# Turning 32 rows of transition factors instead of 16 blocks of input matrix in a state-space preparation

## The chip, the cores and the metric

The kernel runs on one core of a Trainium2 chip. The metric is the device time of one execution in microseconds (us). TensorE is called PE here, VectorE DVE, ScalarE ACT, GpSimd POOL, SyncE SP; PEld is TensorE's weight load.

## The reference

Two layers (`l` = 0, 1) act on `x` [256 tokens, 1024]. Each layer is a SwiGLU feed-forward, a mixer and a second feed-forward, each added to the residual and normalised. The part around the change is the state-space branch of the mixer, cut here to what matters:

```python
def ssm_branch(u, lam_re, lam_im, log_dt, b_re, b_im, c_re, c_im, d_skip, w_glu):
    ...
    dt = jnp.exp(log_dt.astype(f32))[:, None]
    a_bar = jnp.exp(lam * dt)
    b_bar = ((a_bar - 1.0) / lam)[:, :, None] * lax.complex(b_re.astype(f32), b_im.astype(f32))
    c_mat = lax.complex(c_re.astype(f32), c_im.astype(f32))
    bu = jnp.einsum('blgh,gph->blgp', u32.astype(jnp.complex64), b_bar)
    ...
    _, states = lax.associative_scan(combine, (a_seq, bu), axis=1)
    y = jnp.einsum('blgp,ghp->blgh', states, c_mat).real \
        + d_skip.astype(f32).reshape(N_GROUPS, SSM_GROUP) * u32
```

There are 32 groups of 16 channels with 64 complex states each. A complex number takes two planes (`v` = 0 real, 1 imaginary). `a` is `a_bar` and `g` is the step factor `(a_bar - 1) / lam`, one of each per state.

## The kernel before, in words

All weights stream from HBM in tiles of 128x1024 f32. SP loads them into four `raw` slots; ACT makes the high part `whi` (L450) and DVE the remainder `wlo` (L1289), in rings of eight tiles. PE multiplies high by high, high by low and low by high (L777 to L779 and L835, L839). A slot of the ring comes free when PE has used the tile (`pe_used`).

A feed-forward has 11 up chunks (`feature_chunk`, four tiles each) and then a down stage of 22 tiles. When PE has done a chunk, ACT and DVE sum, gate and split it. Their order is written out by hand and has four splits of later weight tiles in it: DVE L1289 twice (the pair), L1327, L1330, L1289, L1335, L1289, L1340; the last one increments `h_split`. The chunks use two sets of PSUM banks, and the last chunk (number 10) lies in banks 0, 1, 6 and 7. The down stage sums in banks 2 to 5; its step `k` is 12 matmuls of 128x512, for both halves of the tokens, and begins while ACT and DVE still work on chunk 10. It is followed by `late_pass`, the normalisation and the transposition of `x` for the next stage.

The constants of the state-space branch are made during the feed-forward ahead of the mixer that uses them: during the first feed-forward of layer 0 for layer 0, and during the second feed-forward of layer 0 for layer 1 (`prepare(l)` on POOL). POOL computes `a` and `g` in [128 states, 16] form, then for four quarters `q` the input matrix `b_bar = g*b` and the product `a*b_bar`, then `a*c`, each by `cmul` (six operations of 128x128). Then it doubles the tables `tab_c` and `tab_s` of cosines and sines seven times; the last two stages work on 128x512 elements at a time, into the scratch tile `h`. `op` (L1709) issues a POOL operation and lets POOL wait for it. After `prepare`, the same queue computes `rstd` (L1733), which the normalisation waits for.

The state input product `ssm_in` needs these matrices with the channels on the partitions. So in the down stage, after step `k` = 5 (`TURN_B_AT`), PE turns 16 blocks of 128x128 (`turn_b`, L965) into banks 0, 1, 6, 7, after a wait for `h_split` of chunk 10; ACT copies them to `b_t` in four pieces (L502). After step 9 (`DIRECT_AT`), PE makes the term `c*b_bar` of even steps in 32 small products (`direct_terms`, L976), which DVE copies to `k0_t` (L1428).

Of the kernel before, what the change touches and what calls it, by code (L numbers as in the profile page):

```python
# [13 lines left out]
P = 128  # L14
# [89 lines left out]
def build(nc, A, out):  # L104
# [65 lines left out]
    b_bar = place("b_bar", [P, NQ, 2, P])  # L170
# [40 lines left out]
    bias_rows = nc.dram_tensor("bias_rows", (N_HEADS, 512), F32, kind="Internal").ap()  # L211

# [6 lines left out]
    for name in ("first_landed first_hi first_lo hi_done split_done pe_used rest_done ident_landed const_landed affine_landed const_ready tok_ready "  # L219
                 "xt_done xh_done x_ready up_done silu_done h_ready ht_done hh_done h_split acc_done "  # L220
                 "var_ready rstd_ready dve_chain pool_chain out_done bias_built bias_stored "
                 "tab_ready gate_low up_low gate_sum gate_silu up_sum up_h par_landed b_landed c_landed d_landed lam_ready "
                 "angle_ready sincos_ready bbar_ready bt_done bt_ready ct_ready k0_done k0_ready ca_ready "
                 "proj_done proj_read pt_done pt_read bu_done bu_read decay_ready scan_done states_ready y_used "
                 "idx_done relu_done weighted idx_added mask_ready mask_set s_done neg_max_ready exp_done prt_done prt_read "
                 "pv_done inv_ready prob_ready yah_done ya_split bra_read y_sum gelu_done yh_done y_split gm_done "
                 "tanh_done glu_ready ysh_done ys_split brs_done bra_done merged_ready mt_done mh_done m_split").split():
        S[name] = sem(name)
# [101 lines left out]

    def bar(q, v):

        return b_bar[:, q, v, :] if v < 2 else b_raw[:, v - 2, 4 * q:4 * q + 4, :].rearrange("p j n -> p (j n)")
# [6 lines left out]
    with block:  # L340
# [102 lines left out]
        def _(act):  # L443
# [70 lines left out]
            def ffn(f, s0, prep):  # L514
                for c in range(OLD_C):
                    token_chunk(f, s0 + 4 * c, c)
                    if c == 1 and prep is not None:
                        prepare_angles(prep)
                h_hi(f, OLD_C - 1)
                for c in range(OLD_C, PEEL):  # L520
                    feature_chunk(0, f, s0 + 4 * c, c, c % 2)
                with act.Fori(0, LOOP_I) as i:
                    for e in range(2):
                        feature_chunk(i, f, s0 + 4 * (PEEL + e), 2 * i + PEEL + e, (PEEL + e) % 2)
                for k in range(HK - RING):
                    splits(s0 + UP_Q + RING + k, 1)
                    if prep is not None and TURN_B_AT <= k < TURN_B_AT + NQ:
                        prepare_b(prep, k - TURN_B_AT)
# [245 lines left out]
        def _(pe):  # L774
# [146 lines left out]
            def late_pass(f, s, k0, n, ah, al, stage, prep):  # L921
# [37 lines left out]
            def turn_b(l, f):  # L959

                pe.wait_ge(S["bbar_ready"], NQ * (l + 1))
                pe.wait_ge(S["h_split"], steps(f, NC_UP - 1) + 1)
                for q in range(NQ):
                    for v in range(4):
                        ins = nc.tensor.transpose(ps[:, TURNED_B[q], v * P:v * P + P], bar(q, v), ident[:, :])  # L965
                    ins.then_inc(S["bt_done"], 1)

            def direct_terms(l):

                pe.wait_ge(S["bt_ready"], NQ * (l + 1))  # L970
                pe.wait_ge(S["ct_ready"], l + 1)
                for q in range(NQ):
                    for v in range(2):
                        for r in range(4):
                            rows = slice(32 * r, 32 * r + 32)
                            ins = nc.tensor.matmul(ps[rows, 0, 32 * q:32 * q + 32], b_bar[:, q, v, rows],  # L976
# [3 lines left out]
            def ffn(f, stage, s0, following, prep):  # L980
# [11 lines left out]
                for k in range(HK - RING):  # L992
# [21 lines left out]
            def ssm_in(l, half):  # L1014

                if half == 0:
                    pe.wait_ge(S["pt_read"], 4 * l + 2)
                    pe.wait_ge(S["bt_ready"], NQ * (l + 1))
# [253 lines left out]
        def _(dve):  # L1272
# [145 lines left out]
            def negate_c(l):  # L1418

                dve.wait_ge(S["c_landed"], 16 * (l + 1))  # L1420
                nc.vector.tensor_scalar(c_t[:, 1, :, :], c_t[:, 1, :, :], -1.0, None, ALU.mult
# [10 lines left out]
            def ffn(f, s0, prep):  # L1432
# [12 lines left out]
                for k in range(HK - RING):  # L1445
                    splits(s0 + UP_Q + RING + k, 1)
                    if prep is not None and k == DIRECT_AT:
                        prepare_k0(prep)
# [251 lines left out]
        def _(pool):  # L1700
# [48 lines left out]
            def prepare(l):  # L1749
# [28 lines left out]
                pool.dma_start(c_t[:, 0:2, :, :], A["ssm_c_rows"][l]).then_inc(S["c_landed"], 16)  # L1778
# [7 lines left out]
                def cmul(dr, di, ar_, ai_, br, bi, sign=1, done=None):  # L1786

                    nc.gpsimd.tensor_tensor(dr, ar_, br, ALU.mult)
                    op(product, ai_, bi, ALU.mult)
                    op(dr, dr, product, ALU.subtract if sign == 1 else ALU.add)  # L1790
                    nc.gpsimd.tensor_tensor(di, ar_, bi, ALU.mult)
                    op(product, ai_, br, ALU.mult)
                    op(di, di, product, ALU.add if sign == 1 else ALU.subtract, done)
# [3 lines left out]

                def prepare_b(q):

                    js = slice(4 * q, 4 * q + 4)  # L1800

                    def bb(v):
                        return bar(q, v).rearrange("p (j n) -> p j n", j=4)

                    cmul(bb(0), bb(1), col(16, js), col(17, js), b_raw[:, 0, js, :], b_raw[:, 1, js, :])
                    cmul(bb(2), bb(3), col(11, js), col(12, js), bb(0), bb(1), 1, S["bbar_ready"])
                    pool.wait_ge(S["bbar_ready"], NQ * l + q + 1)
# [47 lines left out]
                while n < HALF:  # L1855
# [71 lines left out]
TURN_B_AT, DIRECT_AT = 5, 9  # L1927
TURNED_B = [0, 1, 6, 7]
# [5 lines left out]
def ssm_layout(inputs):  # L1934
# [15 lines left out]

    log_dt = np.broadcast_to(np.asarray(inputs["ssm_log_dt"]).reshape(DEPTH, NJ, 2).transpose(0, 2, 1)[:, :, None, :],
# [3 lines left out]
    return {"ssm_params": params, "ssm_d_cols": d_cols, "ssm_b_rows": blocks("ssm_b_re", "ssm_b_im"),  # L1955
# [46 lines left out]
```

## Time and profile before

| what | value |
|---|---|
| time, median of 3 runs | 1106.94 us (1106.74 to 1107.53) |
| the profiled execution's own time | 1107.71 us |
| its span | 1105.9 us |
| granted TensorE clock | 0.998 |
| PE, DVE, ACT, POOL busy | 99%, 71%, 53%, 35% of the span |
| PE in the chain that ended last | 91% of the span |
| HBM read | 207.02 MB, 188 GB/s over the span |

Matmuls overlap in the pipeline, so a row of PE has a duration of 0.39 us while the next one starts 0.23 us later. Costs on PE are read from the differences of start times. "Busy" of DVE and POOL holds the time in which an operation stands still in the engine.

### The profile page before, as it was taken

To read this page: it belongs to the slowest core of one execution; us is meant where nothing else is said; L and a number is where in the kernel's file an instruction comes from. 1 tells how busy PE (TensorE), PEld (TensorE's weight loads), DVE (VectorE), ACT (ScalarE), POOL (GpSimd) and SP (SyncE) were. 2 spreads that over 40 slices of the span, in tenths; PEclk is the share of its full clock that TensorE was granted. 3 is DMA by queue.
4 is the path that set the end of the run, shared out by engine and by line. 5 is a ranking of instruction groups with operands and counts; after the bars stand their busy time and mean duration, and the time that the engine had idled before them with its cause. 6 is when DMAs were issued, how large, how long until landed. Compare 5 with 4: busy or idle time off the path is not lost.

```text
span 1105.9 us, 18440 instructions
## 1 busy us (share of the span) xinstructions
PE 1095.6 (99%) x6411; PEld 929.5 (84%) x6411; DVE 780.6 (71%) x1085; ACT 586.6 (53%) x841; POOL 384.2 (35%) x536
## 2 busy tenths in 40 slices
PE   9999999999999999999999999999999999999997
PEld 7888888997788888888888888889877888888886
DVE  6766676789978866777576667477897787566744
ACT  6555543574873555555345555336748645555540
POOL 3989893107600289989000000011274000000001
PEclk9999999999999999999999999999999999999999
DMA  9866763744575576666466666636545666657651
GB/s 291 269 186 203 253 209 113 229 121 130 158 229 190 173 252 194 190 219 216 124 204 198 183 209 210 224 92 211 168 123 153 209 199 211 192 182 214 204 183 38
DMA packets 158655, 208.96 MB, mean 189 GB/s; under 512 B 12760, under 2 KB 107128, under 8 KB 158592
## 3 DMA queue, kind: packets, MB, share of 16 engines
q1 hardware_dynamic: 155232, 202.29, 57.8%
q10 hardware_dynamic: 2592, 3.67, 1.3%
q0 software_dynamic: 768, 2.17, 0.5%
q8 instruction: 38, 0.62, 0.2%
q14 instruction: 25, 0.20, 0.1%
HBM read 207.02 MB, written 1.06 MB: 188 GB/s over the span
## 4 chain that ended last, share of the span: by engine, by line
PE 91%; DVE 4%; issue 2%; ACT 2%; DMA 1%; POOLq 0%; POOL 0%; DVEq 0%; SPq 0%; ACTq 0%
PE ps L835 24%; PE ps L777 15%; PE ps L779 15%; PE ps L778 15%; PE ps L839 12%; DVE wlo L1289 2%; PE ps L849 1%; PE ps L1166 1%; DMA raw<-in_w_in 1%; PE ps L1168 1%; PE ps L1169 1%; PE ps L791 1%; PE ps L1029 1%; DVE score L1503 1%; PE ps L1081 1%
## 5 line engine op out<-in xcount | busy, mean ns | idle before, releaser
L1289 DVE TENSOR_TENSOR wlo<-raw,whi 128x1024 fp32r<-128x1024 f32 (+1 forms) x371 | 470.0, 1287 | 199.0 <-ACT whi L450 196.1
L450 ACT CAST whi<-raw 128x1024 fp32r<-128x1024 f32 (+1 forms) x371 | 377.4, 1043 | 226.1 <-PE ps L779 134.3
L835 PE MATMUL ps<-x_hl,whi 128*128 128x512 f32 x1152 | 362.5, 396 | 0.0
L839 PEld LDWEIGHTS ps<-x_hl,wlo 128*128 128x128 f32 x1152 | 216.4, 188 | 51.1
L839 PE MATMUL ps<-x_hl,wlo 128*128 128x256 f32 x1152 | 226.5, 278 | 0.0
L1733 POOL TENSOR_TENSOR rstd<-var_eps,cst 128x1 f32<-128x1 f32 x12 | 18.3, 1527 | 542.3 <-DVE var_eps L1355 533.2
L835 PEld LDWEIGHTS ps<-x_hl,whi 128*128 128x128 f32 x1152 | 175.7, 189 | 0.3
L777 PE MATMUL ps<-whi,x_hl 128*128 128x512 f32 (+1 forms) x400 | 156.6, 392 | 0.0
L778 PE MATMUL ps<-wlo,x_hl 128*128 128x512 f32 (+1 forms) x400 | 153.1, 383 | 0.0
L779 PE MATMUL ps<-whi,x_hl 128*128 128x512 f32 (+1 forms) x400 | 153.1, 383 | 0.0
L777 PE MATMUL ps<-whi,hh 128*128 128x512 f32 (+1 forms) x355 | 138.2, 389 | 0.0
L779 PE MATMUL ps<-whi,hl 128*128 128x512 f32 (+1 forms) x355 | 137.5, 387 | 0.0
L778 PE MATMUL ps<-wlo,hh 128*128 128x512 f32 (+1 forms) x355 | 137.5, 387 | 0.0
L777 PEld LDWEIGHTS ps<-whi,x_hl 128*128 128x128 f32 x400 | 75.1, 188 | 17.1 <-issue 3.6
L779 PEld LDWEIGHTS ps<-whi,x_hl 128*128 128x128 f32 x400 | 75.1, 188 | 14.7
L778 PEld LDWEIGHTS ps<-wlo,x_hl 128*128 128x128 f32 x400 | 75.2, 188 | 13.4
L779 PEld LDWEIGHTS ps<-whi,hl 128*128 128x128 f32 x355 | 66.7, 188 | 13.6
L777 PEld LDWEIGHTS ps<-whi,hh 128*128 128x128 f32 x355 | 66.7, 188 | 13.4
L778 PEld LDWEIGHTS ps<-wlo,hh 128*128 128x128 f32 x355 | 66.7, 188 | 13.2
L486 ACT COPY silu<-ps 128x512 f32<-128x512 f32 x36 | 21.1, 587 | 79.1 <-PE ps L839 79.1
L492 ACT CAST hh<-ps 128x512 f32 (+1 forms) x36 | 21.1, 588 | 73.3 <-DVE ps L1335 73.3
L1709 POOL TENSOR_TENSOR small<-small 128x16 f32<-128x16 f32 x102 | 48.2, 472 | 7.9
(206 smaller groups left out, 1370.8 us busy)
## 6 DMA issues: line engine op xcount, KB each, us to landing
raw<-in_ffn_w_up SPq DMA_DIRECT2D x351, 256.0 KB, 3.6
raw<-in_ffn_w_down SPq DMA_DIRECT2D x176, 256.0 KB, 3.3
raw<-in_w_in SPq DMA_DIRECT2D x128, 256.0 KB, 3.4
raw<-in_w_branch SPq DMA_DIRECT2D x32, 256.0 KB, 3.2
raw<-in_w_out SPq DMA_DIRECT2D x32, 256.0 KB, 3.9
bias_g<-bias_rows ACTq DMA_DIRECT2D x16, 192.0 KB, 3.9
raw<-in_w_in SPq DMA_DIRECT2D x16, 148.0 KB, 2.2
affine<-in_ln_g SPq DMA_DIRECT2D x4, 512.0 KB, 5.9
```

What stands on the lines that cost most here:

```text
L450: nc.scalar.copy(whi[:, s % RING, 0:w], raw[:, s % RAW, 0:w]).then_inc(S["hi_done"], 1)
L486: nc.scalar.copy(silu[:, :, :], halves(b, 0)[1]).then_inc(S["gate_low"], 1)
L492: nc.scalar.copy(hh[:, bass.ds(2 * c, 2), :], halves(b, 1)[0]).then_inc(S["hh_done"], 1)
L777: nc.tensor.matmul(o, ah, bh, start=start, stop=False)
L778: nc.tensor.matmul(o, ah, bl, start=False, stop=False)
L779: return nc.tensor.matmul(o, al, bh, start=False, stop=stop)
L791: ins = nc.tensor.transpose(ps[:, XT[i] + half, (k % 4) * P:(k % 4 + 1) * P], x[:, i, k * P:(k + 1) * P], ident[:, :])
L835: nc.tensor.matmul(ps[:, bank, :], w(whi, s + q, at, at + P), x_hl[:, k, :, :], start=k == 0, stop=False)
L839: ins = nc.tensor.matmul(ps[:, bank, 0:SEQ], w(wlo, s + q, at, at + P), xh[:, k, :], start=False, stop=k == KT - 1)
L1289: nc.vector.tensor_tensor(wlo[:, s % RING, 0:w], raw[:, s % RAW, 0:w], f32(whi[:, s % RING, 0:w]), ALU.subtract).then_inc(S["split_done"], 1)
L1709: ins = nc.gpsimd.tensor_tensor(o, a, b, f)
L1733: nc.gpsimd.tensor_tensor(rstd[:, i, :], var_eps[:, i, :], cst[:, 0:1], ALU.pow).then_inc(S["rstd_ready"], 1)
```

## The change: what it does

The step factor `g` goes to the output matrix: `g*c` takes the place of `c`, and the raw `b` that of `b_bar`. So the direct terms need no input matrix made by POOL. `b` is passed a second time by the host, already turned (`ssm_b_cols`, 512 KB a layer), and loaded straight into `b_t`. Of the products, `a*b` is still needed in turned form: POOL writes `a` (16 columns real, 16 imaginary) into `tmp`, PE turns that once, ACT copies the 32 rows and stores them in HBM (`a_rows`, 16 KB), and four DMAs from POOL's queue read them back, each to 32 partitions. POOL then multiplies in six operations of 128x512. The turn comes after step 2 of the down stage (`TURN_A_AT`), with the direct terms right behind it; DVE reads these after its split of step 3.

```diff
-                for q in range(NQ):
-                    for v in range(4):
-                        ins = nc.tensor.transpose(ps[:, TURNED_B[q], v * P:v * P + P], bar(q, v), ident[:, :])
-                    ins.then_inc(S["bt_done"], 1)
+                pe.wait_ge(S["a_ready"], l + 1)
+                pe.wait_ge(S["h_split"], steps(f, NC_UP - 1) + 1)
+                nc.tensor.transpose(ps[:, 1, 0:P], tmp[:, :], ident[:, :]).then_inc(S["at_done"], 1)
...
-                    if prep is not None and k == TURN_B_AT:
-                        turn_b(prep, f)
-                    if prep is not None and k == DIRECT_AT:
+                    if prep is not None and k == TURN_A_AT:
+                        turn_a(prep, f)
                         direct_terms(prep)
...
-                pe.wait_ge(S["bt_ready"], NQ * (l + 1))
-                pe.wait_ge(S["ct_ready"], l + 1)
+                pe.wait_ge(S["b_landed"], 16 * (l + 1))
+                pe.wait_ge(S["cg_ready"], NQ * (l + 1))
...
-                        pe.wait_ge(S["bt_ready"], NQ * (prep + 1))
+                        pe.wait_ge(S["at_read"], prep + 1)
...
-            def prepare_b(l, q):
-                act.wait_ge(S["bt_done"], NQ * l + q + 1)
-                nc.scalar.copy(b_t[:, q, :, :], ps[:, TURNED_B[q], :].rearrange("p (v n) -> p v n", v=4)
-                               ).then_inc(S["bt_ready"], 1)
+            def store_a(l):
+                act.wait_ge(S["at_done"], l + 1)
+                nc.scalar.copy(tmp[0:2 * NJ, :], ps[0:2 * NJ, 1, 0:P]).then_inc(S["at_read"], 1)
+                act.wait_ge(S["at_read"], l + 1)
+                act.dma_start(a_rows, tmp[0:2 * NJ, :]).then_inc(S["a_stored"], 16)
...
+                pool.dma_start(b_t[:, :, 0:2, :], A["ssm_b_cols"][l]).then_inc(S["bc_landed"], 16)
...
-                pool.wait_ge(S["b_landed"], 16 * (l + 1))
                 pool.wait_ge(S["ct_ready"], l + 1)
                 for q in range(NQ):
-                    prepare_b(q)
-                for q in range(NQ):
                     js = slice(4 * q, 4 * q + 4)
-                    cmul(c_t[:, 2, js, :], c_t[:, 3, js, :], col(11, js), col(12, js), c_t[:, 0, js, :],
-                         c_t[:, 1, js, :], -1, S["ca_ready"])
-                    pool.wait_ge(S["ca_ready"], NQ * l + q + 1)
+                    cmul(c_t[:, 0, js, :], c_t[:, 1, js, :], col(16, js), col(17, js), c_t[:, 2, js, :],
+                         c_t[:, 3, js, :], product, -1, S["cg_ready"])
+                    pool.wait_ge(S["cg_ready"], NQ * l + q + 1)
+                op(tmp[:, 0:NJ], ar, k(14), ALU.mult)
+                op(tmp[:, NJ:2 * NJ], ai, k(14), ALU.mult, S["a_ready"])
...
+                pool.wait_ge(S["tab_ready"], l + 1)
+                pool.wait_ge(S["a_stored"], 16 * (l + 1))
+                for r in range(4):
+                    src = bass.AP(a_rows.tensor, r * P, [[0, 32], [NJ * P, 2], [4 * P, NQ], [1, P]])
+                    pool.dma_start(at_t[32 * r:32 * r + 32, :, :, :], src).then_inc(S["a_landed"], 16)
+                for q in range(NQ):
+                    js = slice(4 * q, 4 * q + 4)
+                    cmul(c_t[:, 2, js, :], c_t[:, 3, js, :], col(11, js), col(12, js), c_t[:, 0, js, :],
+                         c_t[:, 1, js, :], product, -1, S["ca_ready"])
+                    pool.wait_ge(S["ca_ready"], NQ * l + q + 1)
+                pool.wait_ge(S["a_landed"], 64 * (l + 1))
+                pool.wait_ge(S["bc_landed"], 16 * (l + 1))
+                t = h[:, 1, :, :].rearrange("p t n -> p (t n)").rearrange("p (q n) -> p q n", q=NQ)
+                cmul(b_t[:, :, 2, :], b_t[:, :, 3, :], at_t[:, 0, :, :], at_t[:, 1, :, :], b_t[:, :, 0, :],
+                     b_t[:, :, 1, :], t, 1, S["bt_ready"])
...
-TURN_B_AT, DIRECT_AT = 5, 9
-TURNED_B = [0, 1, 6, 7]
+TURN_A_AT, READ_K0_AT = 2, 3
```

How instructions move, first on PE, in the down stage of the feed-forward that holds the preparation. Before, step 5 is followed by:

```order
L779 MATMUL ps<-whi,hl 128x512
L965 MATMUL ps<-ident,b_bar 128x128 [waits h_split,bbar_ready]
L965 MATMUL ps<-ident,b_bar 128x128
L965 MATMUL ps<-ident,b_raw 128x128 x2
...
L777 MATMUL ps<-whi,hh 128x512 [waits split_done]
...
L976 MATMUL ps<-c_t,b_bar 32x32 [waits ct_ready,bt_ready]
L976 MATMUL ps<-c_t,b_bar 32x32 x31
```

where the last two rows follow step 9. With the change, step 2 is followed by:

```order
L777 MATMUL ps<-whi,hl 128x512
L961 MATMUL ps<-ident,tmp 128x128 [waits h_split,a_ready]
L971 MATMUL ps<-c_t,b_raw 32x32 [waits cg_ready,b_landed]
L971 MATMUL ps<-c_t,b_raw 32x32 x31
L775 MATMUL ps<-whi,hh 128x512 [waits split_done]
```

The wait for `h_split` has moved ahead by three steps, the small products by seven. On POOL, in `prepare`, the last table operation was followed at once by `rstd`:

```order
L1868 TENSOR_TENSOR tab_s<-tab_c,small 128x8x64 [waits pool_chain]
L1709 TENSOR_TENSOR h<-tab_s,small 128x512
L1709 TENSOR_TENSOR tab_s<-tab_s,h 128x8x64 [waits pool_chain]
L1733 TENSOR_TENSOR rstd<-var_eps,cst 128x1 [waits var_ready] x2
L1709 TENSOR_TENSOR h_st<-spare 128x16 [waits tok_ready]
```

and now stand between them (the 24 operations of `a*c` shortened to their first two):

```order
L1703 TENSOR_TENSOR tab_s<-tab_s,h 128x8x64 [waits pool_chain]
L1863 DMA at_t<-a_rows 32x8x128 [waits a_stored,tab_ready]
L1863 DMA at_t<-a_rows 32x8x128 x3
L1783 TENSOR_TENSOR c_t<-small,c_t 128x128
L1703 TENSOR_TENSOR tmp<-small,c_t 128x128
...
L1783 TENSOR_TENSOR b_t<-at_t,b_t 128x4x128 [waits bc_landed,a_landed,ca_ready]
L1703 TENSOR_TENSOR h<-at_t,b_t 128x512
L1703 TENSOR_TENSOR b_t<-b_t,h 128x4x128 [waits pool_chain]
L1786 TENSOR_TENSOR b_t<-at_t,b_t 128x4x128 [waits pool_chain]
L1703 TENSOR_TENSOR h<-at_t,b_t 128x512
L1703 TENSOR_TENSOR b_t<-b_t,h 128x4x128 [waits pool_chain]
L1727 TENSOR_TENSOR rstd<-var_eps,cst 128x1 [waits var_ready] x2
```

Ahead of the tables, POOL's 72 operations of 128x128 have become 24, so that the tables start earlier, and work that was ahead of them now lies behind.

## Rows read from the trace of the kernel before

**Rows 1.** The page's busy time, share of the span and instructions of each engine.
```profile
PE 1095.6 (99%) x6411; PEld 929.5 (84%) x6411; DVE 780.6 (71%) x1085; ACT 586.6 (53%) x841; POOL 384.2 (35%) x536
```
**Rows 2.** The longest wait of PE: line, releaser: us in total, times, longest.
```profile
PE ps L1259 <- DVE k_t L1662: 1.3, 1, 1.3
```
**Rows 3.** Timeline of PE, layer 0, around the 16 transpositions: start us, duration us.
```profile
146.16 0.38 PE L965 MATMUL ps<-ident,b_bar 128*128 128x128 f32 x2
...
147.83 0.47 PE L777 MATMUL ps<-whi,hh 128*128 128x512 f32 x1
```
**Rows 4.** Timeline of PE, layer 0, around the direct terms.
```profile
158.92 0.76 PE L976 MATMUL ps<-c_t,b_bar 128*32 128x32 f32 x64
159.62 0.51 PE L777 MATMUL ps<-whi,hh 128*128 128x512 f32 x1
```
**Rows 5.** Timeline of PE, the end of step 2: layer 0, then layer 1's preparation.
```profile
137.99 0.39 PE L777 MATMUL ps<-whi,hh 128*128 128x512 f32 x1
...
499.68 0.39 PE L777 MATMUL ps<-whi,hh 128*128 128x512 f32 x1
```
**Rows 6.** Timeline of DVE on chunk 10, layer 0; in brackets the idle time before.
```profile
128.93 2.62 DVE L1289 TENSOR_TENSOR wlo<-raw,whi 128x1024 fp32r<-128x1024 f32 x2
131.47 0.69 DVE L1327 TENSOR_TENSOR ps<-ps,silu 128x512 f32<-128x512 f32 x1
...
137.48 1.49 DVE L1289 TENSOR_TENSOR wlo<-raw,whi 128x1024 fp32r<-128x1024 f32 x1 [1.71 <-ACT whi L450]
138.89 0.68 DVE L1340 TENSOR_TENSOR hl<-ps,hh 128x512 f32 x1
```
**Rows 7.** The same of layer 1's preparation.
```profile
489.25 2.90 DVE L1289 TENSOR_TENSOR wlo<-raw,whi 128x1024 fp32r<-128x1024 f32 x2
...
494.63 2.02 DVE L1289 TENSOR_TENSOR wlo<-raw,whi 128x1024 fp32r<-128x1024 f32 x1 [1.00 <-ACT whi L450]
...
498.96 2.06 DVE L1289 TENSOR_TENSOR wlo<-raw,whi 128x1024 fp32r<-128x1024 f32 x1 [1.71 <-ACT whi L450]
500.95 0.68 DVE L1340 TENSOR_TENSOR hl<-ps,hh 128x512 f32 x1
```
**Rows 8.** DVE L1289, ns min/median/max, in 60:142, 142:175 and 494:528 us.
```profile
L1289 DVE TENSOR_TENSOR wlo<-raw,whi x31: 1207/1297/1485, 60.3 to 141.8; 128x1024 fp32r<-128x1024 f32 x31
L1289 DVE TENSOR_TENSOR wlo<-raw,whi x12: 1225/1516/2266, 141.8 to 172.0; 128x1024 fp32r<-128x1024 f32 x12
L1289 DVE TENSOR_TENSOR wlo<-raw,whi x13: 1228/1750/2311, 494.6 to 525.5; 128x1024 fp32r<-128x1024 f32 x13
```
**Rows 9.** Timeline of POOL, layer 0: products, tables, `rstd`.
```profile
63.73 0.40 POOL L1788 TENSOR_TENSOR b_bar<-small,b_raw 128x128 f32<-128x128 f32 x1
...
96.82 0.40 POOL L1788 TENSOR_TENSOR c_t<-small,c_t 128x128 f32<-128x128 f32 x1
...
112.34 0.24 POOL L1865 TENSOR_TENSOR tab_c<-tab_c,small 128x16 f32<-128x16 f32 x1
...
156.11 1.05 POOL L1865 TENSOR_TENSOR tab_c<-tab_c,small 128x512 f32<-128x512 f32 x1
...
174.16 1.29 POOL L1709 TENSOR_TENSOR tab_s<-tab_s,h 128x512 f32<-128x512 f32 x1
183.70 1.54 POOL L1733 TENSOR_TENSOR rstd<-var_eps,cst 128x1 f32<-128x1 f32 x1 [8.24 <-DVE var_eps L1355]
```
**Rows 10.** The same of layer 1's preparation: first and last table operation.
```profile
463.65 0.23 POOL L1865 TENSOR_TENSOR tab_c<-tab_c,small 128x16 f32<-128x16 f32 x1
...
525.11 1.30 POOL L1709 TENSOR_TENSOR tab_s<-tab_s,h 128x512 f32<-128x512 f32 x1
```
**Rows 11.** POOL's issue of one DMA: count | us in all, mean ns | idle before.
```profile
L1778 POOL DMA_DIRECT2D c_t<-in_ssm_c_rows x2 | 1.1, 538 | 0.0
```
**Rows 12.** DMA issues of POOL: KB each, median us to landing.
```profile
c_t<-in_ssm_c_rows POOLq DMA_DIRECT2D x2, 512.0 KB, 7.4
bias_rows<-bias_sb POOLq DMA_DIRECT2D x1, 16.0 KB, 4.7
```

More of the change, by code:

```diff
@@ L169, in build @@
     b_raw = place("b_raw", [P, 2, NJ, 32])
-    b_bar = place("b_bar", [P, NQ, 2, P])
+    at_t = place("at_t", [P, 2, NQ, P])
     tmp = place("tmp", [P, P])
@@ L211, in build @@
     bias_rows = nc.dram_tensor("bias_rows", (N_HEADS, 512), F32, kind="Internal").ap()
+    a_rows = nc.dram_tensor("a_rows", (2 * NJ, P), F32, kind="Internal").ap()
     raw_landed = [sem(f"raw_landed{i}") for i in range(RAW)]
@@ L526, in ffn @@
                     splits(s0 + UP_Q + RING + k, 1)
-                    if prep is not None and TURN_B_AT <= k < TURN_B_AT + NQ:
-                        prepare_b(prep, k - TURN_B_AT)
+                    if prep is not None and k == TURN_A_AT:
+                        store_a(prep)
             def proj_read(l, c, t):
@@ L975, in direct_terms @@
                             rows = slice(32 * r, 32 * r + 32)
-                            ins = nc.tensor.matmul(ps[rows, 0, 32 * q:32 * q + 32], b_bar[:, q, v, rows],
+                            ins = nc.tensor.matmul(ps[rows, 0, 32 * q:32 * q + 32], b_raw[:, v, 4 * q + r, :],
                                                    c_t[:, v, 4 * q + r, :], start=v == 0, stop=v == 1)
@@ L996, in ffn @@
                     ins.then_inc(S["pe_used"], 1)
-                    if prep is not None and k == TURN_B_AT:
-                        turn_b(prep, f)
-                    if prep is not None and k == DIRECT_AT:
+                    if prep is not None and k == TURN_A_AT:
+                        turn_a(prep, f)
                         direct_terms(prep)
@@ L1017, in ssm_in @@
                     pe.wait_ge(S["pt_read"], 4 * l + 2)
-                    pe.wait_ge(S["bt_ready"], NQ * (l + 1))
+                    pe.wait_ge(S["bt_ready"], l + 1)
                     pe.wait_ge(S["proj_read"], 2 * NPROJ * l + 4)
@@ L1420, in negate_c @@
                 dve.wait_ge(S["c_landed"], 16 * (l + 1))
-                nc.vector.tensor_scalar(c_t[:, 1, :, :], c_t[:, 1, :, :], -1.0, None, ALU.mult
+                nc.vector.tensor_scalar(c_t[:, 3, :, :], c_t[:, 3, :, :], -1.0, None, ALU.mult
                                         ).then_inc(S["ct_ready"], 1)
@@ L1446, in ffn @@
                     splits(s0 + UP_Q + RING + k, 1)
-                    if prep is not None and k == DIRECT_AT:
+                    if prep is not None and k == READ_K0_AT:
                         prepare_k0(prep)
@@ L1784, in prepare, with cmul @@
                 product = tmp[:, :].rearrange("p (j n) -> p j n", j=4)
-                def cmul(dr, di, ar_, ai_, br, bi, sign=1, done=None):
+                def cmul(dr, di, ar_, ai_, br, bi, t, sign=1, done=None):
                     nc.gpsimd.tensor_tensor(dr, ar_, br, ALU.mult)
-                    op(product, ai_, bi, ALU.mult)
-                    op(dr, dr, product, ALU.subtract if sign == 1 else ALU.add)
+                    op(t, ai_, bi, ALU.mult)
+                    op(dr, dr, t, ALU.subtract if sign == 1 else ALU.add)
                     nc.gpsimd.tensor_tensor(di, ar_, bi, ALU.mult)
-                    op(product, ai_, br, ALU.mult)
-                    op(di, di, product, ALU.add if sign == 1 else ALU.subtract, done)
+                    op(t, ai_, br, ALU.mult)
+                    op(di, di, t, ALU.add if sign == 1 else ALU.subtract, done)
                 def col(n, js):
                     return m(n)[:, js].unsqueeze(2).to_broadcast([P, 4, 32])
[L1798 to L1807, printed above, removed]
                 def square(dr, di, sr, si_):
@@ L1949, in blocks, with turned @@
         return rows.reshape(DEPTH, P, 2, NJ, 2 * SSM_GROUP)
+    def turned(rows):
+        return rows.reshape(DEPTH, P, 2, NQ, 4, 32).transpose(0, 4, 5, 3, 2, 1).reshape(DEPTH, P, NQ, 2, P)
+    b_rows = blocks("ssm_b_re", "ssm_b_im")
     log_dt = np.broadcast_to(np.asarray(inputs["ssm_log_dt"]).reshape(DEPTH, NJ, 2).transpose(0, 2, 1)[:, :, None, :],
```

11 lines of the change are left out of this document (4 added, 7 removed).

## The prediction

> **What bounds the kernel now.** I read the page's busy shares first: PE is busy for 99% of the span [rows 1]. Then the list of waits: the longest wait of PE in the whole execution is 1.3 us, and that is at the start [rows 2]. So PE sets the end in every stage, whatever ACT, DVE and POOL do beside it. An edit is worth what it takes from PE's own queue, less each moment in which it makes PE wait where it did not wait before. The next views are therefore timelines: PE's at the place of the edit, then those of the engines that release the wait which has moved there, and last POOL's, whose work is moved about.
>
> **What PE saves.** The first transposition starts at 146.16 us and the next weight product at 147.83 [rows 3]. That is 1.67 us, and the product behind them takes 0.47 us where the others take 0.39 or 0.40, 0.08 more. So 16 transpositions cost 1.75 us, 0.11 us each, and one is left: 1.64 us less for each layer, 3.3 us for both. The direct terms (0.70 us from their start to that of the next product, [rows 4]) keep their number and shapes and only move; I cost that at nothing. Their inputs are there: `g*c` is done by about 80 us (below) and needed at 138.
>
> **What the moved wait costs.** Both the old and the new turn wait for `h_split` of chunk 10, because they write to a bank that chunk 10 fills. DVE's last operation on that chunk starts at 138.89 us and takes 0.68, so the chunk is split at 139.57 [rows 6]. The old turn at 146.16 found it long done. The new one stands behind step 2, which is issued in full when step 3 starts in the old trace, at 137.99 us [rows 5]. As it is, PE would stand for 139.57 - 137.99 = 1.6 us. In layer 1's preparation the chunk is split at 500.95 + 0.68 = 501.63 [rows 7] and step 2 ends at 499.68 [rows 5]: 1.95 us. Queued behind that wait on PE are the direct terms and all weight products; nothing can go past it. I add 0.2 us each time for the restart, since the transposition's weight load can't be hidden under a running product; no row shows this, the spacing of transpositions (0.11 us) is a bound from below and a product of 0.39 one from above.
>
> **How POOL changes these two waits.** In front of the tables, POOL has 48 operations fewer: the block of `b` products ran from 63.73 to 96.82 us, 33.1 us, and is gone; the block of `c` products (96.82 to 112.34, 15.5 us) is replaced by one of `g*c` of the same shapes [rows 9]. New are two operations of 128x16 and one DMA issue of 0.54 us [rows 11], about 1.1 us together. So all tables come 32 us earlier. Their last stage, on tiles of 128x512, ran from 156.11 to 175.45 and will run from about 124 to 143.5, right over the chain of chunk 10. In layer 1's preparation the tables ended at 525.11 + 1.30 = 526.4 [rows 10] and will end at 494.4, near the middle of that chain.
>
> This matters because DVE's splits are slower beside such POOL operations: the median of L1289 is 1.30 us before 142 us, and 1.52 and 1.75 us in the two stretches with large table operations, up to 2.27 and 2.31 [rows 8]. In layer 0 five splits lie on the path to `h_split` from 126 us on: one of chunk 9, the pair ahead of L1327 (2.62 us together, and L1327 starts when DVE is free of it), and two inside the chain, 1.49 us for the last of them [rows 6]. They take about 1.4 us each now. At 1.65, between the two medians, they take 0.26 more each, 1.3 in all: the wait is 1.6 + 1.3 = **2.9 us**. The bounds are 1.6 (no split is slower) and 1.6 + 5 x 0.65 = 4.8 (each takes 2.02 to 2.06, as the two of rows 7 do).
>
> In layer 1's preparation it is the other way round for two of them: the two splits inside the chain took 2.02 and 2.06 us beside large POOL operations [rows 7] which will be over. At 1.30 they give back 1.5 us, while the pair ahead (2.90 us) and the one before it take some 0.5 more. That is 1.95 + 0.5 - 1.5 = 0.95. POOL's end (494.4) is close to the first of the two (494.63), so part of its share may stay; I take **1.2 us**, with bounds of 0.5 and 2.3 (the pair at 2.0 each, +1.1, and only the second split freed, -0.75).
>
> **What lies beside.** POOL must not be late for `rstd`. After the tables it waits for the store of `a`: turn at about 141, copy, a store that by the one small store in the trace lands 4.7 us after issue [rows 12], so 147. Four issues at 0.54 [rows 11] are 2.2, `a*c` is 15.5 again, and six operations of 128x512 are half of the last table stage (19.3 us for twelve), 9.7. End: 174.4 us, where the tables ended at 175.45 and POOL then sat idle for 8.24 us until 183.70 [rows 9]. The read-back has the 15.5 us of `a*c` to land, against 7.4 us for 512 KB [rows 12]. So the DMA detour costs nothing, as long as this gap of 9 us holds. ACT loses four copies and gets a small one and an issue; PE waits for it nowhere. DVE's read of the direct terms stands behind its split of step 3's ring slot, which comes after the terms are done. The added load of 512 KB a layer competes with weight tiles for some 2 us; splits run eight tiles ahead of PE, so I cost it at nothing, with 0.5 us as its upper end.
>
> **The sum.** -3.3 + 2.9 + 1.2 + 2 x 0.2 = **+1.2 us**, on the profiled execution's own 1107.7 us: 1108.9. The median of the three runs is 0.8 below that execution, so as a median it is 1106.94 + 1.2, some 1108.2 us. A measurement of this kernel can tell about 0.2% (2.2 us) from no change, so this counts as no change.
>
> The Trainium skill (SBUF — State Buffer, Who interferes with whom) says that a DVE instruction with two SBUF inputs contends with a POOL instruction that reads SBUF, through one shared read interface that is held as a lock. L1289 has two such inputs, and rows 8 agree in kind: it stretches to 2.3 us, and not only slightly. Taken as a lock on each of the five splits, the rule would make the time that of rival 2.
>
> **The rivals.**
> 1. *The wait is short* (18%). The splits keep their durations, since POOL and DVE happen to alternate: waits of 1.6 and 0.5 us, restart 0.3. Sum -3.3 + 2.4 = -0.9: 1106.0 us. For it: the minimum beside large operations is 1.23 us in both stretches [rows 8]. Against: the medians.
> 2. *Every split stands behind a POOL operation* (16%). Waits of 4.8 and 2.3, restart 0.4. Sum +4.2: 1111.1 us, slower. The place is chunk 10 in layer 0, and it decides from about 3.9 us there on, when the sum passes 2.2. For it: rows 7, where two of two splits took 2 us. Against: a median of 1.52 in the stretch that is moved here.
> 3. *The wait isn't one* (6%). `h_split` comes before step 2 is through, in both layers. Sum -3.3: 1103.7 us, faster. Against it stand both timelines, in which DVE is 1.6 and 1.95 us too late; it needs the change to speed up DVE ahead of both places, and it puts large POOL operations there in layer 0.
> 4. *POOL is late for `rstd`* (5%). If the four broadcast reads cost POOL 5 us each in place of 0.54, or land after 26 us in place of 7.4, the gap of 9 us is used up, and each further us is lost twice, once a layer. At 5 us over it is 10 us: about 1118 us. Nothing like this stands in the rows.
>
> The change could also fail to do what it says: POOL's total work hardly falls (72 small operations become 48, plus six large ones). But that isn't on PE's path, so it decides nothing.
>
> **How the numbers follow.** The forecast has 55%, with 1106.5 to 1110.5 as its own range; 8 of these 55 lie over +2.2 us. Slower by over 0.2%: 16 + 5 + 8 and a rounding = 30%. Faster by over 0.2%: rival 3 and 2% for a short wait that is shorter still: 8%. Within 0.2%: 62%. The range from 1106.0 to 1111.5 takes in the forecast and the greater part of rivals 1 and 2 and leaves out 3 and 4, nearly 2 in 10.
>
> **What would show it.** PE's timeline after step 2 must show a gap ahead of the transposition, released by DVE's split of chunk 10, near 3 us in layer 0 and 1 us in the next; the waits of PE must have a new group of about 4 us. The 16 rows of L965 must have become one of 0.1 us. L1289 must be slower between 126 and 139 us than before, and the large table operations must lie there. POOL must be idle before `rstd` as before. If the gap in layer 0 is 1.6 us or less, the step on DVE's splits is wrong; if PE waits at the transposition of `x`, rival 4 holds; if PE's gap is right and the time is not, the price of the transpositions is wrong.

## The result and the profile after

| | before | changed |
|---|---|---|
| time, median (lowest to highest) | 1106.94 us (1106.55 to 1107.53) | 1111.53 us (1110.11 to 1113.05) |
| profiled execution's own time, span | 1107.71, 1105.9 us | 1112.81, 1111.0 us |

The ratio of the times is 1.0041 [1.0032, 1.0050]: the changed kernel is slower by 4.6 us, which is more than the 0.2% that a measurement tells from no change. It lies at the upper edge of the forecast range (1111.5), 3.4 us above the forecast of +1.2, and in the case to which the prediction gave 30%. As a number it is nearest to rival 2 (1111.1 us), though that rival's waits were not met, as the rows below show. All seven executions are slower than every one before, and they spread over 2.9 us where those of before spread over 1.0.

The page's busy line and PE's longest waits, which answer to [rows 1] and [rows 2]:

```profile
PE 1095.7 (99%) x6381; PEld 928.8 (84%) x6381; DVE 786.6 (71%) x1085; ACT 583.3 (53%) x835; POOL 384.7 (35%) x514
```
```profile
PE ps L961 <- DVE hl L1334: 5.5, 2, 3.6
PE ps L1253 <- DVE k_t L1656: 1.3, 1, 1.3
```

30 of PE's instructions are gone, and yet its busy time is the same to 0.1 us. The new wait is the forecast one (`turn_a`, released by DVE's split of chunk 10), with 5.5 us where 4.1 was forecast. Something else must have made PE's instructions longer. The timeline of PE in layer 0 shows what; it answers to [rows 3] and [rows 5]:

```profile
138.00 0.39 PE L777 MATMUL ps<-whi,hl 128*128 128x512 f32 x1
141.95 0.30 PE L961 MATMUL ps<-ident,tmp 128*128 128x128 f32 x1 [3.57 <-DVE hl L1334]
142.18 1.06 PE L971 MATMUL ps<-c_t,b_raw 128*32 128x32 f32 x64
143.17 0.80 PE L775 MATMUL ps<-whi,hh 128*128 128x512 f32 x1
...
144.62 0.63 PE L775 MATMUL ps<-whi,hh 128*128 128x512 f32 x1
145.05 0.63 PE L776 MATMUL ps<-wlo,hh 128*128 128x512 f32 x1
...
146.02 0.39 PE L776 MATMUL ps<-wlo,hh 128*128 128x512 f32 x1
```

The next product was due at 138.23, so the gap is 3.72 us. Behind it the 32 small products take 0.99 us to the next start, where they took 0.70 [rows 4], and the weight products start 0.43 us apart instead of 0.23 until 145.5. The granted clock, in stretches of 4 us with PE's busy time, says why:

```profile
138.00:142.00 4.00, 0.43 (x3) 1.00 0.39 131
142.00:146.00 4.00, 4.00 (x72) 0.57 0.72 241
146.00:150.00 4.00, 4.00 (x19) 1.00 0.78 228
503.00:507.00 4.00, 2.03 (x71) 1.00 0.47 150
507.00:511.00 4.00, 4.00 (x11) 0.57 0.81 282
511.00:515.00 4.00, 4.00 (x19) 1.00 0.76 240
```

The columns are the stretch, PE's busy time with its instructions, the granted clock, the DMA share and GB/s. Behind each gap the clock is at its lower level (1.2 GHz in place of 2.4) for most of a stretch: 0.57 in the mean. In layer 0 it is low as soon as PE works again. In the other place the small products and the first weight products still run at full speed, and the slow ones begin 1.6 us after PE has started again. In the trace of before it is 1.00 in all six. In layer 1's preparation:

```profile
503.53 0.39 PE L777 MATMUL ps<-whi,hl 128*128 128x512 f32 x1
505.88 0.30 PE L961 MATMUL ps<-ident,tmp 128*128 128x128 f32 x1 [1.97 <-DVE hl L1334]
...
507.69 0.63 PE L775 MATMUL ps<-whi,hh 128*128 128x512 f32 x1
508.12 0.63 PE L776 MATMUL ps<-wlo,hh 128*128 128x512 f32 x1
```

Here the gap is 505.88 - 503.76 = 2.1 us. The lower clock costs 1.4 us in layer 0: 0.3 in the small products, and 1.1 in the weight products until they start 0.23 us apart again. Here it costs 1.6 us: eleven products take 4.20 us from 506.81 to 511.01, and eleven at full clock 2.6. When each instruction of PE is compared with the same one in the trace of before, PE falls back by 3.54 us at the first turn and 2.08 at the second. In both that is gap, plus slow stretch, less transpositions: 3.7 + 1.4 - 1.65 and 2.1 + 1.6 - 1.65, within 0.1. Some 0.5 us came before and between. 1.2 us is given back in layer 1's attention, where the profiled execution of before had a wait of 1.2 us that this one lacks. The sum is +5.0, and the profiled executions differ by 5.1.

Why the first gap is so long stands in DVE's timeline on chunk 10, which answers to [rows 6]:

```profile
127.07 1.23 DVE L1283 TENSOR_TENSOR wlo<-raw,whi 128x1024 fp32r<-128x1024 f32 x1 [1.71 <-ACT whi L447]
...
128.82 3.70 DVE L1283 TENSOR_TENSOR wlo<-raw,whi 128x1024 fp32r<-128x1024 f32 x2
...
134.72 2.14 DVE L1283 TENSOR_TENSOR wlo<-raw,whi 128x1024 fp32r<-128x1024 f32 x1 [1.00 <-ACT whi L447]
...
139.18 2.02 DVE L1283 TENSOR_TENSOR wlo<-raw,whi 128x1024 fp32r<-128x1024 f32 x1 [1.71 <-ACT whi L447]
141.12 0.68 DVE L1334 TENSOR_TENSOR hl<-ps,hh 128x512 f32 x1
```

Chunk 10 is split at 141.80, where it was split at 139.57: 2.2 us later. Read one by one, the five splits take 1.23 us (chunk 9), 1.47 and 2.31 (the pair, merged above into 3.70), 2.14 and 2.02. So three of the five take over 2 us. POOL's timeline beside them, which answers to [rows 9]:

```profile
135.86 1.91 POOL L1848 TENSOR_TENSOR tab_c<-tab_c,small 128x512 f32<-128x512 f32 x1
137.74 1.04 POOL L1703 TENSOR_TENSOR h<-tab_s,small 128x512 f32<-128x512 f32 x1
138.85 1.27 POOL L1703 TENSOR_TENSOR tab_c<-tab_c,h 128x512 f32<-128x512 f32 x1
140.20 1.90 POOL L1851 TENSOR_TENSOR tab_s<-tab_c,small 128x512 f32<-128x512 f32 x1
```

The large table operations lie over the chain as forecast, and they stretch in turn. Those that take 1.04 to 1.3 us where no split is beside them often take 1.9 to 2.3 where one is. The Trainium skill (SBUF — State Buffer, Who interferes with whom) describes such a lock between a two-input DVE instruction and POOL. The trace agrees in kind. Of the 44 splits of this execution that lie for most of their time beside POOL operations of 128x512, 8 take 1.2 to 1.3 us, 15 take 1.35 to 1.75 and 21 take 1.9 to 2.35. The 222 with no POOL operation beside them take 1.2.

### The profile page after: what moved, and what is told of

Read it like the earlier page. It is cut to its first block, busy times and chain, and to the rows that moved or that the text cites. A ratio compares the mean times of both kernels' runs of the same rounds, so it can differ in the third digit from the quotient of the medians.

```text
span 1111.0 us, 18356 instructions
## 1 busy us (share of the span) xinstructions
PE 1095.7 (99%) x6381; PEld 928.8 (84%) x6381; DVE 786.6 (71%) x1085; ACT 583.3 (53%) x835; POOL 384.7 (35%) x514
## 4 chain that ended last, share of the span: by engine, by line
PE 80%; DVE 7%; issue 5%; ACT 4%; DMA 3%; SPq 1%; DVEq 0%; POOLq 0%; POOL 0%; ACTq 0%
PE ps L833 20%; PE ps L775 14%; PE ps L777 14%; PE ps L776 14%; PE ps L837 10%; DVE wlo L1283 3%; ACT whi L447 2%; DMA raw<-in_ffn_w_down 2%; PE ps L1160 1%; DMA raw<-in_ffn_w_up 1%; PE ps L1162 1%; PE ps L1163 1%; PE ps L789 1%; PE ps L1023 1%; DVE score L1497 1%
## 5 line engine op out<-in xcount | busy, mean ns | idle before, releaser
L1283 DVE TENSOR_TENSOR wlo<-raw,whi 128x1024 fp32r<-128x1024 f32 (+1 forms) x371 | 476.2, 1304 | 207.1 <-ACT whi L447 204.5
L1896 POOL TENSOR_TENSOR h_st<-tab_c,gates 128x512 f32<-128x512 f32 x8 | 10.4, 1296 | 114.1 <-DVE wlo L1283 87.4
```

The lines of the kernel that those rows point to most:

```text
L1283: nc.vector.tensor_tensor(wlo[:, s % RING, 0:w], raw[:, s % RAW, 0:w], f32(whi[:, s % RING, 0:w]), ALU.subtract).then_inc(S["split_done"], 1)
```

## Experiments

All these kernels compute what the changed one does, or the one before. "PE gains" or "loses" is said of PE's instructions compared one by one with the same ones in the trace of before. The kernel before was run beside each: 1106.90 us (33 executions) for the first four, 1106.75 (29) for the others.

### The turn three steps later

```diff
-TURN_A_AT, READ_K0_AT = 2, 3
+TURN_A_AT, READ_K0_AT = 5, 6
```

> The changed kernel with the turn and the direct terms after step 5 of the down stage in place of step 2, nothing else. Theory A (the time was lost at the moved wait: a gap on PE, and behind it products at the lower of TensorE's two clocks): step 5 is issued at about 146.2 us, chunk 10 is split at 141.8, so there is no gap and no slow stretch; the time is that of before less 3.3 us, 1103.7 us, and the granted clock is 1.00 in every stretch of the down stage. Theory B (the added DMA load, the store and read-back, or POOL's new order cost PE something elsewhere): the time stays above 1105 us, and PE's waits or products show another place. The rival on POOL being late for rstd: POOL's chain starts some 4 us later than with step 2 and still ends about 3 us before rstd is wanted, so nothing is lost by either theory.

1104.94 us (1103.69 to 1106.46), ratio 0.9980 [0.9971, 0.9989]. Nothing waits at the turn, and the clock stays up. PE's timeline:

```profile
146.70 0.40 PE L777 MATMUL ps<-whi,hl 128*128 128x512 f32 x1
146.94 0.27 PE L961 MATMUL ps<-ident,tmp 128*128 128x128 f32 x1
147.14 0.76 PE L971 MATMUL ps<-c_t,b_raw 128*32 128x32 f32 x64
147.83 0.50 PE L775 MATMUL ps<-whi,hh 128*128 128x512 f32 x1
```

Turn and small products take 0.89 us together. PE gains 1.67 us at each of the two turns, 1.64 forecast. So the transpositions' price is right, and all that made the changed kernel slower than before hangs on the turn's place. The median falls by 1.96 us only, which misses the 1103.7 us expected by 1.2; the transpositions alone give 3.3. Of the rest the trace shows 0.8 us by which PE comes late to the first turn, 0.2 of it from a wait for chunk 9's split. That leaves about the 2.4 us by which the two profiled executions differ; why the medians lie 0.5 us closer stays open. The added DMA load and POOL's new order are in this kernel too, and it is faster than before: neither is what made the changed one slower by itself.

The same kernel was run again with the later ones, to compare within one chip:

> The turn after step 5 once more, to stand beside the kernel with the moved block of a*c on the same chip: 1104.9 us again, within 0.5 us.

1104.27 us (1103.34 to 1107.99), ratio 0.9981 [0.9973, 0.9990]: the same.

### The turn one step later

```diff
-TURN_A_AT, READ_K0_AT = 2, 3
+TURN_A_AT, READ_K0_AT = 3, 4
```

> The changed kernel with the turn after step 3. Step 3 is issued at 141.0 us in layer 0 and 506.5 in the other, chunk 10 is split at 141.8 and 505.7. Theory A: a gap of about 1 us in layer 0 and none in layer 1's preparation; time 1103.7 + 1 = 1104.7 us if so short a gap leaves the clock up, about 1106.2 if the clock falls behind it as it did behind 3.6 and 2.0 us. Theory B: no difference to the changed kernel beyond the gap, 1108 us or more.

1105.01 us (1103.85 to 1105.94), ratio 0.9980 [0.9970, 0.9989]. One step of twelve products, 2.7 us, is enough: no wait for chunk 10 is left, where one of about 1 us was expected in layer 0, and PE gains 1.64 and 1.67 us at the turns. DVE's timeline in layer 0 adds something to the reading above:

```profile
129.70 3.45 DVE L1283 TENSOR_TENSOR wlo<-raw,whi 128x1024 fp32r<-128x1024 f32 x2
135.35 1.22 DVE L1283 TENSOR_TENSOR wlo<-raw,whi 128x1024 fp32r<-128x1024 f32 x1 [1.00 <-ACT whi L447]
138.90 1.23 DVE L1283 TENSOR_TENSOR wlo<-raw,whi 128x1024 fp32r<-128x1024 f32 x1 [1.71 <-ACT whi L447]
```

The same two splits, in the same order of work on POOL, took 2.14 and 2.02 us in the profiled execution of the changed kernel and 1.2 here. Here the chunk is split at 140.72, 0.4 us before PE comes to the turn. A turn after step 2 would have stood 2.3 us. So the length of the gap in the changed kernel can be expected to differ from one execution to the next.

How long a turn after step 2 stands, or would stand, can be read in every trace, those of the later experiments too: it is the time from the end of step 2 to the split of chunk 10. The durations are those of single splits, the pair's two added.

| trace | layer 0: wait | pair, two splits inside the chain | layer 1's preparation: wait |
|---|---|---|---|
| before | 1.57 | 2.70, 1.42, 1.49 | 1.95 |
| wait alone | 1.35 | 2.69, 1.42, 1.47 | 1.15 |
| `a*c` ahead | 2.10 | 2.78, 1.41, 1.30 | 2.29 |
| both edits | 1.47 | 2.79, 1.41, 1.30 | 1.75 |
| changed | 3.57 | 3.78, 2.14, 2.02 | 1.97 |
| turn after step 5 | 2.56 | 3.52, 1.23, 1.23 | 1.99 |
| the same again | 3.64 | 3.77, 1.23, 2.05 | 1.67 |
| turn after step 3 | 2.32 | 3.52, 1.22, 1.23 | 1.98 |
| turn after step 8 | 3.68 | 3.76, 1.23, 2.05 | 1.67 |
| gap filled | 2.54 | 3.52, 1.23, 1.22 | 2.50 |

In the last six, with large table operations over the chain of layer 0, the wait is 2.3 to 3.7 us, 3.05 in the mean. The pair is slower in all six; the two splits inside the chain are slower in some only.

### The wait alone, in the kernel before

```diff
                     ins.then_inc(S["pe_used"], 1)
+                    if prep is not None and k == 2:
+                        pe.wait_ge(S["h_split"], steps(f, NC_UP - 1) + 1)
                     if prep is not None and k == TURN_B_AT:
```

> The kernel before with one wait added on PE: h_split of chunk 10 after step 2 of the down stage; transpositions and direct terms stay where they are. Theory A: gaps of 1.6 us in layer 0 and 2.0 us in layer 1's preparation plus restart, some 0.3 each, and if the clock falls behind such gaps another 1.5 us each: 1106.9 + 4.2 = 1111.1 us with the fall, 1111.1 - 3 = 1108 us without it. Theory B, by which the wait isn't what costs: within 0.1% of before, 1107 to 1108 us.

1109.95 us (1108.76 to 1112.95), ratio 1.0027 [1.0018, 1.0036]. The gaps are those of the old order of POOL:

```profile
138.59 0.39 PE L779 MATMUL ps<-whi,hl 128*128 128x512 f32 x1
140.22 0.50 PE L777 MATMUL ps<-whi,hh 128*128 128x512 f32 x1 [1.24 <-DVE hl L1342]
...
501.57 0.39 PE L779 MATMUL ps<-whi,hl 128*128 128x512 f32 x1
503.00 0.50 PE L777 MATMUL ps<-whi,hh 128*128 128x512 f32 x1 [1.04 <-DVE hl L1342]
```

The first product starts 1.40 and 1.20 us later than it was due, and it takes 0.11 us more until its successor starts. That makes 1.51 and 1.31, together 2.8 of the 3.05 us that the median shows. So the wait costs about 3 us without any change on POOL and with the transpositions as they were. The expected gaps were 1.6 and 2.0 us. In this execution the clock stays at 1.00 behind both. Two of the eleven executions lie 2 and 3 us above the median (1111.86 and 1112.95); the mean clock of the second is 0.997, of all others 0.998 or 0.999.

### `a*c` ahead of the last table stage

```diff
                 while n < HALF:
+                    if 2 * n == HALF:
...
+                        for q in range(NQ):
...
                     step = min(NJ, 4 * P // n)
...
-                for q in range(NQ):
...
                 pool.wait_ge(S["a_landed"], 64 * (l + 1))
```

> The changed kernel with POOL's block of a*c moved ahead of the last table stage (its scratch goes to h). Theory A with the contention of POOL and DVE: the large table operations start at 126 + 16 = 142 us in layer 0, behind the chain of chunk 10, so the splits there take 1.3 to 1.5 us as before the change and the gap shrinks from 3.7 to about 2 us; in layer 1's preparation they start at 494 us, over the chain, and the gap grows from 2.1 to about 3.3 us. The time hardly moves, 1110 to 1112 us; the two gaps are the test. If the contention is not the cause of the longer chain, both gaps stay as they are.

In the diff, `...` stands for the 24 operations of `a*c` and their scratch tile. 1108.08 us (1106.81 to 1110.79), ratio 1.0011 [1.0001, 1.0020]: 3.4 us less than the changed kernel, where hardly any difference (1110 to 1112 us) was expected. In layer 0 small POOL operations lie beside chunk 10. The pair takes 2.78 us, against 3.5 to 3.8 in the table above, and the splits inside the chain 1.41 and 1.30 (DVE's timeline):

```profile
135.35 1.41 DVE L1283 TENSOR_TENSOR wlo<-raw,whi 128x1024 fp32r<-128x1024 f32 x1 [1.00 <-ACT whi L447]
...
139.08 1.30 DVE L1283 TENSOR_TENSOR wlo<-raw,whi 128x1024 fp32r<-128x1024 f32 x1 [1.72 <-ACT whi L447]
```

The gaps are 141.12 - 138.88 = 2.24 us (3.72 in the changed kernel) and 504.98 - 502.54 = 2.44 (2.1). The second was expected to grow to 3.3. There the pair takes 3.98 us beside the large operations, but the two splits inside the chain are at 1.23. That these are short proves little by itself, since they are so beside large operations too in three rows of the table; the pair and the medians carry the reading. The two gaps also show that the clock doesn't follow from the length alone (PE, stretches of 4 us, columns as above):

```profile
138.00:142.00 4.00, 1.91 (x70) 1.00 0.43 150
142.00:146.00 4.00, 4.00 (x23) 0.59 0.81 275
502.00:506.00 4.00, 1.72 (x70) 1.00 0.49 154
506.00:510.00 4.00, 4.00 (x18) 1.00 0.80 251
```

The shorter gap is followed by the lower clock, the longer one isn't. The profiled execution is the slowest of the ten, 2.7 us above their median. Of the others three have a mean clock of 0.997 or less, and six 0.998 or more.

### Both edits

> The turn after step 5, and POOL's block of a*c ahead of the last table stage. Theory A with contention: with the turn at step 5 the trace lost 0.5 us before the down stage of layer 0, where PE waited for the split of chunk 9, which large POOL operations had made late; here these lie at 144 us and later, so that wait is gone and the time is 0.5 us under the kernel with the turn at step 5 alone, 1103.5 to 1104.5 us. If the 0.5 us was chance, both kernels take the same. POOL ends at about 181 us, still ahead of rstd's point of need (184 us); should it be late, PE waits at the transposition of x and the time is above that of the turn at step 5 alone.

The turn after step 5 and `a*c` ahead of the last stage: 1103.91 us (1103.16 to 1104.82), ratio 0.9974 [0.9966, 0.9983]. It has the lowest median of all and beats both kernels. Its interval doesn't separate it from the turn after step 5 alone (0.9981 beside it).

### The turn six steps later

```diff
-TURN_A_AT, READ_K0_AT = 2, 3
+TURN_A_AT, READ_K0_AT = 8, 9
```

> The changed kernel with the turn after step 8. PE has no gap at the turn, as with step 5, but POOL's read-back can start only when a is stored, at about 158 us in layer 0 and 519 in the other, and its last product then ends near 188 and 548 us, 2 to 4 us after rstd is wanted. The theory that POOL's gap ahead of rstd is the limit of the detour: PE waits at the transposition of x, 1 to 4 us a layer, and the time is 1105 + 2 to 8, some 1109 us. The theory that the detour never reaches PE: 1105 us, as with step 5.

1108.81 us (1107.02 to 1110.68), ratio 1.0019 [1.0010, 1.0028]. Now what rival 4 describes happens, POOL late for `rstd`, though by the late store and not by slow reads. POOL waits 22 us for the store in layer 0, and `rstd` follows the last product of `b_t` without idle time at 188.33. PE then waits at the transposition of `x` (2.55 us idle), and the products behind it run at the lower clock again:

```profile
186.90 0.39 PE L777 MATMUL ps<-whi,hl 128*128 128x512 f32 x1
189.84 1.57 PE L789 MATMUL ps<-ident,x 128*128 128x128 f32 x8 [2.55 <-DVE x L1360]
191.06 0.78 PE L775 MATMUL ps<-whi,hh 128*128 128x512 f32 x1
191.63 0.63 PE L776 MATMUL ps<-wlo,hh 128*128 128x512 f32 x1
```

PE gains 1.67 us at each turn here too and loses 4.54 in layer 0 and 1.63 in layer 1's preparation afterwards. So the turn has a window: it waits for nothing after steps 3 and 5, and costs on either side of that. Step 5 is close to its end: POOL's idle time before `rstd` in layer 0 is 10.7 us with the turn after step 2, 4.9 after step 3, and 0.8 and 0.35 in the two traces of step 5.

### The gap filled with products

```diff
                 pe.wait_ge(S["a_ready"], l + 1)
+                for _ in range(4 if l == 0 else 2):
+                    nc.tensor.matmul(ps[:, ACC[0], :], at_t[:, 0, 0, :],
+                                     f32(hh[:, 0:2, :]).rearrange("p k n -> p (k n)"), start=False, stop=False)
                 pe.wait_ge(S["h_split"], steps(f, NC_UP - 1) + 1)
...
+                op(at_t[:, 0, 0, :], k(9, P), k(9, P), ALU.mult)
```

> The changed kernel, turn after step 2, with PE busy in the gap: ahead of the wait it multiplies a tile of zeros by 512 columns in f32 into the running sum, 4 times in layer 0 and twice in the other (some 0.85 us each, so that they end before the wait does); one POOL operation makes the zeros. If the slow stretch behind the gap comes from PE standing idle, the granted clock stays 1.00, the products behind the turn keep 0.23 us, and the time is 3 us under the changed kernel's, 1108.0 to 1108.8 us, though the wait itself is as long. If the slow stretch has another cause (the small products, the transposition), the time stays at 1110.5 to 1112 us.

The turn stays after step 2, and PE adds products of zeros to a sum while it would stand. 1110.40 us (1109.99 to 1110.99), ratio 1.0033 [1.0020, 1.0046]. PE in layer 0, and the clock in the stretches from 138 and 502 us:

```profile
139.51 3.59 PE L961 MATMUL ps<-hh,at_t 128*128 128x512 f32 x8
142.94 0.27 PE L964 MATMUL ps<-ident,tmp 128*128 128x128 f32 x1
143.14 0.76 PE L974 MATMUL ps<-c_t,b_raw 128*32 128x32 f32 x64
143.84 0.50 PE L775 MATMUL ps<-whi,hh 128*128 128x512 f32 x1
```
```profile
138.00:142.00 4.00, 4.00 (x14) 1.00 0.39 132
142.00:146.00 4.00, 4.00 (x77) 1.00 0.70 219
502.00:506.00 4.00, 3.31 (x38) 1.00 0.38 132
506.00:510.00 4.00, 4.00 (x76) 1.00 0.84 229
```

The products hold PE for 3.43 us in place of the gap of 3.72, and the clock stays up. In layer 1's preparation 2.56 us pass before the turn, 0.69 of them idle, and again no slow product follows. At the two turns PE loses 1.77 and 0.96 us where the changed kernel loses 3.54 and 2.08. These are 3.4 and 2.6 us of delay less the transpositions: the slow stretches are gone. Yet the median falls by 1.1 us only, where 3 were expected, and the intervals of the two ratios overlap. All five executions lie within 1.0 us, the seven of the changed kernel within 2.9.

The mean granted clock of each execution, which was taken with its time, tells why. A stretch of 4 us at 0.57 takes 0.0015 off the mean of a whole execution. The profiled executions agree: 0.996 with two such stretches, 0.997 with one, 0.998 or 0.999 with none.

| kernel | executions with 0.998 or 0.999 | with 0.997 or less |
|---|---|---|
| before, all 62 beside the experiments | 62: 1106.07 to 1108.51 | none |
| changed | 2: 1110.11, 1110.39 | 5: 1110.33 to 1113.05 |
| wait alone | 10: 1108.76 to 1111.86 | 1: 1112.95 |
| `a*c` ahead | 6: 1106.81 to 1108.15 | 4: 1108.60 to 1110.79 |
| turn after step 8 | 6: 1107.02 to 1108.99 | 4: 1109.75 to 1110.68 |
| gap filled | 5: 1109.99 to 1110.99 | none |
| turn after step 3, after step 5 (twice), both edits | 43: 1103.16 to 1106.46 | 1: 1107.99 |

The filled kernel takes what the changed one takes when its clock stays up. So the filling removes the lower clock and its spread, and leaves the wait. What the expectation had wrong is the size: the median of the changed kernel holds some 1.3 us of lower clock, and not 3.

## Why the forecast was right in mechanism and low in size

The term that was too small is that of the moved wait. It was sized at 2.9 and 1.2 us with a restart of 0.2 each, 4.5 us in all. The gaps measured 3.7 and 2.1, and behind them the lower clock cost 1.4 and 1.6 us: 8.8 us in the profiled execution. That the time still lies in the range is partly luck: the range reached so far up for rival 2's waits of 4.8 and 2.3 us, which were 3.57 and 1.97, and a cost that was not in the prediction filled the rest.

- **Transpositions, -3.3 us.** Right: -1.64 to -1.67 us for each layer in all profiled executions with the turn at a later place.
- **PE too early as it is, 1.6 and 1.95 us.** Right as a reading of that one trace, somewhat high in general: with the wait alone in the kernel before, the gaps were 1.40 and 1.20 us. The wait alone cost 3.05 us in the median.
- **Splits beside large table operations, five at +0.26 us.** About right in the mean, low for the profiled execution. There the wait in layer 0 is 3.57 us where 2.9 was forecast and 4.8 was the upper bound: the chain from chunk 9 to chunk 10 is 2.3 us longer, and chunk 9 was done 0.3 us earlier against PE. Over the six traces with this order on POOL it is 2.3 to 3.7 us, 3.05 in the mean. What 1.65 us for each split hid is the spread: they take 1.2 to 1.5 or about 2, and which of the two changes from one execution to the next. The rows on the very same chain in layer 1's preparation [rows 7] were the nearest, and held both kinds: 2.02, 2.06, and a pair that was 1.21 and 1.77.
- **Layer 1's preparation, 1.2 us.** Low by 0.8, and by 0.5 to 1.3 in all six traces. The two splits inside the chain did come down to 1.23 us, as expected, and from chunk 9 to chunk 10 the chain is 1.35 us shorter. But DVE came into it late. Before, it was done with chunk 9 2.2 us ahead of the down stage's first product (489.33 against 491.51), now 0.8 us (494.78 against 495.58). POOL's operations of 128x512 now begin at 466.7 us, where they began at 493.5, and the splits beside them take up to 2.35 us where they took 1.2 to 1.65. The prediction counted only the five splits nearest to the wait.
- **Restart, 0.2 us each.** Here lay the missed term. The transpositions started 0.15 us after the split, so the restart itself was well sized. But a bound from the rows at full clock left out that the clock itself can fall behind a gap. No row of before shows it, because PE has no gap over 1.3 us there; a bound of twice the time for some products would have been due.
- **The DMA detour, nothing.** Right. The store lands 2.9 us after its issue (4.7 forecast), the read-back 5.8 us after its own, and POOL idles 10.7 us before `rstd` in both layers. In layer 1's preparation POOL also waits 11.3 us for the store, which the prediction had not looked at; it costs nothing either. Moving the turn by six steps shows that this cover is not endless.

The Trainium skill (TensorE: Matmul & The Clock Gate, HAM oscillation) says that waits of TensorE between bursts of matmuls can throw the clock back to half, so that the next burst starts slow. The trace agrees with its 0.57 behind both gaps, though not every gap of this size was followed by it (2.44 us with `a*c` ahead was not). It was not weighed in the prediction, where it spoke against the change.

The medians add up without the profile. The change with a turn that doesn't wait gives -2.0 and -2.5 us (two comparisons). The wait alone gives +3.05. Together some +0.6 to +1.1, and the kernel in which the small `a*c` lies over chunk 10 gives +1.2. The change itself gives +4.6: the 3.4 us between them come only where the turn waits *and* the large table operations lie over the chain that it waits for. The mean clocks divide them roughly. The two executions of the changed kernel with the clock up lie at 1110.25 in the mean, the six with `a*c` ahead at a median of 1107.8. So some 2.5 us are there without the lower clock, and about 1 us of the medians' difference is the clock. Two executions are few, and the waits read from the traces (2.10 and 2.29 us with `a*c` ahead, 3.05 and 1.96 in the mean of the six) account for under 1 us of the 2.5; the rest stays open.

## What to carry to other kernels

When a wait is moved to an earlier place on the engine that sets the end, price the chain that releases it with the neighbours that it will have after the change. Start far enough back to see how late the releasing engine enters the chain, and take both values of a contended operation rather than their median. Add to each new gap on PE what the products behind it cost at the lower clock. A step of PE that needs another engine's result has a window bounded by that result and by its own consumer; here one step of 2.7 us turned +4.6 into -1.9 us, and a turn after step 8 lost again.

## What was unexpected

- A gap of 2.1 us on a PE that was busy before and after was followed by some seven products at the lower clock, 0.43 us apart instead of 0.23; so was one of 2.24 us, while one of 2.44 us wasn't, nor were those of 1.2 and 1.4 us in the execution that was profiled. So for gaps of this size the clock was not settled by their length. It fell in some executions of a kernel and not in others, and those in which it did are the slow end of each kernel's times. What else decides was not found.
- Filling the gap with products that do nothing kept the clock at 1.00.
- Beside POOL operations of 128x512, the DVE split of 128x1024 takes anything from 1.2 to 2.35 us, with few between 1.5 and 1.9, and they take about 0.9 us longer or none: both sides pay. How long the same split takes changes from one execution to the next (2.14 and 1.22 us for the first inside chunk 10's chain).
